# Attention weights times values: a two-part sum against a plain float32 one in two column halves, with dense and grid heads in turn

## The chip, the core and the metric

One core of one Trainium2 chip runs the whole program. The metric is the device time in microseconds (us), from one launch to its end. The core has five engines that run side by side and wait for each other by semaphores: TensorE (PE: matmuls, with PEld for its weight loads), VectorE (DVE), ScalarE (ACT), GpSimd (POOL) and SyncE (SP, which here only starts DMA transfers).

## The reference

The kernel computes a two-layer encoder over 1024 positions of width 1024. In each layer a norm and a projection give queries, keys and values for 16 heads of three kinds; each kind's output is normed, projected and added to x; then comes an MLP.

```python
def reference(x, g_mix, w_in, q_norm, w_uq, kv_norm, w_ukv, rpb, ...):
    for l in range(DEPTH):                                   # DEPTH = 2
        h = rms_norm(x, g_mix[l])
        proj = h @ w_in[l]
        ...
        o_a = dense_attention(qa, ka, kva[..., QK_NOPE:])    # 6 heads, 1024 x 1024, latent keys
        o_b = dilated_sliding_attention(...)                 # 6 heads, three windows with one softmax
        o_c = neighbourhood_attention(..., rpb[l])           # 4 heads on a 16 x 64 grid, bias rpb
        mixed = jnp.concatenate([rms_norm(o_a), rms_norm(o_b), rms_norm(o_c)], axis=-1)
        x = x + mixed @ w_out[l]
        h2 = rms_norm(x, g_mlp[l])
        x = x + jnp.square(jax.nn.relu(h2 @ w_mlp_in[l])) @ w_mlp_out[l]
    return rms_norm(x, g_final)

def dense_attention(q, k, v):
    ...
    sc = jnp.einsum('bqhd,bkhd->bhqk', q_blk, k) * scale
    p = jax.nn.softmax(sc, axis=-1)
    return jnp.einsum('bhqk,bkhd->bqhd', p, v)               # the weighted sum
```

All of it is float32, and each head is 64 wide.

## The kernel before

**Split numbers.** Most matmuls are of type float32r. So that nothing is lost, an operand is kept as two float32r parts: `hi`, which ACT rounds from the float32 value by a copy, and `lo`, which DVE makes as value minus `hi` (helper `rest`, L824). The transposes of probabilities (L1264) and the `merge` (L1304) are plain float32 matmuls.

**Stages of a layer.** Projections (L1174; three passes over hi and lo), then attention, then the norm of its output, the output projection, a second norm and the MLP. The layer loop is a hardware loop (`Fori`) on every engine, so that a wait's target is a register's value worked out with `l`.

**Attention** is a list of 128 items per layer: a head and a block of 128 queries. `HEADS` sets their order: 6 heads of kind A (dense), 6 of kind B (dilated, computed densely with a table of biases), 4 of kind C (grid). A and B items (96 per layer, "dense" below) have 1024 keys, C items (32 per layer) 384. PE's order is written out in the loop of L1308 to L1316. In step i it does:

- `scores(i)` (L1247 for dense, L1238 for grid) into one of two pairs of PSUM banks
- `turns(i - 2)` (L1264): the probabilities of item i-2, turned in blocks of 128x128, 8 for a dense item (two groups of four), 3 for a grid item (one group)
- in every fourth step, `merge` of a block of four items that is done
- `weigh(b, part)`, the weighted sum: a block b of four items is done in four parts, one per step, so that step i holds a quarter of the block of items 4 to 8 places back

In between, DVE takes the row maximum (A: L974) or adds the bias and takes the minimum (B, C: L986), ACT takes the exponential (L716), for C items DVE divides by the sum (L992, L994), and after the turn ACT copies a group to `pT` hi (L706) and DVE writes `pT` lo (L824).

**The weighted sum.** Values lie in DRAM as 128 columns per head, 64 hi and 64 lo, and the stationary operand of a matmul is a tile of 128 keys by these 128 columns. For each tile of keys two matmuls follow, one for each part of `pT`. Rows 0 to 63 of the result hold what the values' hi gives, rows 64 to 127 what lo gives. ACT copies it to `oT` (L734, L742), and `merge` turns it back and adds the two halves, since its moving operand `pair` is two unit matrices of 64 stacked.

**Values on their way to DRAM.** In the projections each of 24 tiles of values per layer is copied to `vst` hi by ACT (L656) and to lo by DVE (L824, L933), and POOL starts the store (L543).

**Grid heads.** SP loads for each C head 6 pieces of features, 16 pieces of values (L420) and two halves of the bias (L381, 768 KB each); a half is loaded when the bias buffer is free. ACT negates the bias, one item's 384 columns at a time (L726), two items ahead.

## Time and profile before

| | us |
|---|---|
| median of 3 runs | 2985.09 |
| lowest and highest run | 2983.09, 2988.78 |
| profiled execution: span, first to last instruction | 2983.4 |
| profiled execution: attention of layer 0, dense items (291.7 to 588) | 296.3 |
| profiled execution: attention of layer 0, grid items (588 to 657) | 69.0 |

Only the span of the profiled execution is recorded, without what lies around it. It is 1.7 us below the median of the runs. The engines' busy shares of the span are PE 96%, DVE 58%, ACT 36%, POOL 1%. A PE that is busy is not always fast: its clock is granted in two levels, shown as a share of full speed, and the mean over the span is 0.983.

How to read the rows further on: a row of instruction groups has line, engine, operation, operands, shape, count, busy time in all, mean duration of one, and the idle time of the engine just before them with what ended it. PE's matmuls overlap each other, so the duration of one is longer than the step from one to the next; a step is read from the starts of two rows of the timeline, divided by the count. A float32 (not float32r) matmul that is no transpose stands in the trace as two records; L1304 is written 256 times and has 512.

### The profile page before, as it was taken

How to read it: one execution, taken by the hardware profiler on the slowest of the kernel's cores; microseconds unless marked ns; L12 is line 12 of the kernel's file. 1: busy time of each engine (PE TensorE's matmuls, PEld its weight loads, DVE VectorE, ACT ScalarE, POOL GpSimd, SP SyncE). 2: the span in 40 equal slices, each digit the busy share in tenths (PEclk: the TensorE clock that was granted, in tenths of full speed). 3: DMA queues.
4: the chain of work that ended last, by engine and by line, in shares of the span. 5: the costliest groups of instructions: out<-in, count | busy, mean ns of one | idle time of the engine just before them, and what ended most of it. 6: DMA issues, size and time to landing. Idle time of an engine off the chain costs nothing.

```text
span 2983.4 us, 43794 instructions
## 1 busy us (share of the span) xinstructions
PE 2876.5 (96%) x14640; PEld 2454.8 (82%) x14640; DVE 1733.5 (58%) x3038; ACT 1081.0 (36%) x2056; POOL 26.5 (1%) x53
## 2 busy tenths in 40 slices
PE   7999999979999999999999999999799999999998
PEld 7998888867888888888799988887688888888886
DVE  5642778865555455455656337788655555455457
ACT  5332768864311111111334236777632111111113
POOL 0000000000000000000000000000000000000000
PEclk9999999989999999999999999999799999999999
DMA  5657534463111111111146573336530111111111
GB/s 192 185 179 181 123 84 94 103 160 120 43 43 56 42 42 56 42 56 49 59 166 200 168 182 88 87 93 142 133 108 29 56 42 56 42 43 55 42 61 69
DMA packets 194043, 281.45 MB, mean 94 GB/s; under 512 B 47184, under 2 KB 153296, under 8 KB 184144
## 3 DMA queue, kind: packets, MB, share of 16 engines
q1 hardware_dynamic: 190032, 262.56, 30.5%
q0 software_dynamic: 3840, 16.78, 1.5%
q8 instruction: 87, 1.43, 0.2%
q14 instruction: 84, 0.69, 0.1%
HBM read 208.50 MB, written 70.78 MB: 94 GB/s over the span
## 4 chain that ended last, share of the span: by engine, by line
PE 83%; DVE 5%; issue 5%; DMA 4%; ACT 2%; DVEq 1%; ACTq 0%; SPq 0%; POOLq 0%
PE ps L1349 23%; PE ps L1174 19%; PE ps L1364 17%; PE ps L1247 7%; PE ps L1264 6%; PE ps L1293 6%; DMA biasC<-in_bias_c 2%; PE ps L1304 2%; PE ps L1211 1%; PE ps L1142 1%; DVE hn L841 1%; DVE x L1095 1%; DMA values<-vst 1%; DVE vbuf L1082 1%; ACT rbuf L774 1%
## 5 line engine op out<-in xcount | busy, mean ns | idle before, releaser
L1364 PE MATMUL ps<-w_dn,hid 128*128 128x512 f32 x3072 | 713.1, 391 | 1.4
L1349 PE MATMUL ps<-hT,w_up 128*128 128x512 f32 x3072 | 702.6, 389 | 3.1 <-DVE hT L824 3.1
L1364 PEld LDWEIGHTS ps<-w_dn,hid 128*128 128x128 f32 x3072 | 573.5, 188 | 132.1 <-DVE x L1095 14.0
L1349 PEld LDWEIGHTS ps<-hT,w_up 128*128 128x128 f32 x3072 | 576.1, 188 | 123.1 <-DVE hT L824 3.6
L1174 PE MATMUL ps<-ws,hT 128*128 128x384 f32 (+3 forms) x3072 | 607.8, 356 | 6.8 <-DVE ws L824 3.5
L1174 PEld LDWEIGHTS ps<-ws,hT 128*128 128x128 f32 x3072 | 535.8, 190 | 53.6 <-issue 6.0
L1095 DVE TENSOR_TENSOR x<-ps,x 128x512 f32<-128x512 f32 x512 | 342.8, 689 | 223.8 <-PE ps L1364 223.4
L1082 DVE TENSOR_TENSOR vbuf<-rbuf 128x512 f32<-128x512 f32 x128 | 88.6, 692 | 367.5 <-ACT rbuf L774 367.5
L824 DVE TENSOR_TENSOR pT<-ps,pT 128x512 fp32r<-128x512 f32 (+1 forms) x448 | 281.6, 664 | 33.5 <-ACT pT L706 33.4
L706 ACT ACTIVATE pT<-ps 128x512 fp32r<-128x512 f32 (+1 forms) x448 | 240.2, 581 | 152.1 <-PE ps L1264 148.0
L774 ACT ACTIVATE rbuf<-ps 128x512 f32<-128x512 f32 x128 | 76.6, 598 | 550.6 <-PE ps L1349 550.6
L760 ACT ACTIVATE w_dn<-raw 128x2048 fp32r<-128x2048 f32 x32 | 61.3, 1917 | 559.0 <-PE ps L1364 559.0
L716 ACT ACTIVATE prob<-ps,a_nm 128x1024 f32<-128x1024 f32 (+1 forms) x256 | 252.5, 986 | 13.5 <-DVE a_nm L986 8.5
L1264 PE MATMUL ps<-ident,prob 128*128 128x128 f32 x1728 | 239.3, 278 | 10.2 <-DVE prob L994 9.4
L1264 PEld LDWEIGHTS ps<-ident,prob 128*128 128x128 f32 x1728 | 204.1, 143 | 51.2 <-issue 20.0
L1247 PE MATMUL ps<-head 128*128 128x512 f32 x768 | 225.7, 395 | 8.6 <-DVEq L935 6.1
L1293 PE MATMUL ps<-pT,head 128*128 128x512 f32 x768 | 224.6, 414 | 0.5 <-DVE pT L824 0.5
L1247 PEld LDWEIGHTS ps<-head 128*128 128x128 f32 x768 | 144.0, 189 | 42.7 <-DVEq L935 6.9
L974 DVE TENSOR_REDUCE a_nm<-ps 128x1 f32<-128x1024 f32 x96 | 117.5, 1224 | 73.3 <-PE ps L1247 72.9
L1293 PEld LDWEIGHTS ps<-pT,head 128*128 128x128 f32 x768 | 130.1, 189 | 17.1 <-issue 0.9
L986 DVE CUSTOM_DVE_ANT_0 ps<-ps,tabB 128x1024 f32<-128x1024 f32 x96 | 118.1, 1230 | 38.5 <-PE ps L1247 36.6
L1142 PE MATMUL ps<-ident,hn 128*128 128x128 f32 x448 | 70.4, 305 | 42.8 <-DVEq L843 22.5
(84 smaller groups left out, 2108.1 us busy)
## 6 DMA issues: line engine op xcount, KB each, us to landing
raw<-in_wstream SPq DMA_DIRECT2D x76, 1024.0 KB, 4.8
head<-feats SPq DMA_DIRECT2D x192, 256.0 KB, 5.8
feats<-tst SPq DMA_DIRECT2D x128, 192.0 KB, 2.6
values<-vst POOLq DMA_DIRECT2D x32, 384.0 KB, 3.1
head<-values SPq DMA_DIRECT2D x24, 512.0 KB, 3.9
biasC<-in_bias_c SPq DMA_DIRECT2D x16, 768.0 KB, 7.3
raw<-in_wstream SPq DMA_DIRECT2D x12, 768.0 KB, 5.7
x_park<-x SPq DMA_DIRECT2D x16, 512.0 KB, 9.1
```

Of the source, the lines that this page charges most:

```text
L706: act.activation(pT[:, b % 2, HI, k0:k0 + nk, (it % 4) * P:(it % 4 + 1) * P], ps[:, 4 + g % 2, 0:nk * P].rearrange("p (k s) -> p k s", s=P ...
L716: act.activation(prob[:, i % 2, 0:wd], s_in, ACT.Exp, bias=a_nm[:, i:i + 1], scale=1.0 if kind == "A" else -1.0, accum_out=a_den[:, i:i + ...
L824: return dve.tensor_tensor(out_lo, full, words(hi), ALU.subtract)
L986: dve.tensor_tensor_reduce(out=s_in, in0=s_in, in1=bias, scale=1.0, scalar=-NEG, op0=ALU.add, op1=ALU.min, accum_out=a_nm[:, i:i + 1])\
L1082: dve.tensor_tensor(vbuf[:, k % 2, :], rbuf[:, k % 2, :], rbuf[:, k % 2, :], ALU.mult)
L1095: dve.tensor_tensor(x[:, s, cols], ps[:, 2 + m % 4, :], x[:, s, cols], ALU.add)\
L1174: last = pe.matmul(out_, a, b, start=(n == 0), stop=(n == len(mms) - 1))
L1247: last = pe.matmul(ps[:, b0 + kh, :], a, b, start=(k == 0), stop=(k == len(mm) - 1))
L1264: last = pe.transpose(ps[:, 4 + g % 2, j * P:(j + 1) * P], prob[:, i % 2, c:c + P], ident[:, :])
L1293: last = pe.matmul(bank, hb[:, 4096 + kt * P:4096 + (kt + 1) * P], pT[:, b % 2, w, kt, :], start=(part == 0 and kt == 0 and w == 0), stop= ...
L1349: last = pe.matmul(ps[:, k % 2, :], w_up[0 if first else 1][:, w1, kt, ft * P:(ft + 1) * P], hT[:, w2, kt, sh * 512:(sh + 1) * 512], start ...
L1364: last = pe.matmul(ps[:, 2 + m % 4, :], hid[slot][:, w1, ft, s * P:(s + 1) * P], w_dn[1 if last_group else 0][:, w2, ft, nh * 512:(nh + 1) ...
```

## The change

Four edits in one.

**1. The weighted sum in plain float32.** Values are stored as 64 float32 columns per head (`vst`, `values`, `v_dense`, `v_grid`), without hi and lo, and `pT` has one float32 part. A matmul of `weigh` has a stationary operand of 64 columns, and its result goes to rows 0 to 63 or to rows 64 to 127 of the bank, in turns: even tiles of keys to the one, odd tiles to the other (grid items: column blocks 0 and 1 to the one, 2 and 3 to the other). In the built program these matmuls carry a tile of the array of 128x64, at column 0 or 64; all others use the whole array. `merge` is as before: it now adds the sum over even tiles to that over odd ones. A group of turned probabilities is copied once, by ACT (`on_act`: first group of a dense item, every group of a grid item) or by DVE (second group of a dense item). The values' tiles on their way to DRAM are copied by ACT alone.

**2. Order of heads.** A0 C0 A1 C1 A2 C2 A3 C3 A4 A5 B0 ... B5.

**3. The bias** is negated by GpSimd, a half of four items (1536 columns) in one instruction.

**4. The layer loop** is a Python loop on all engines, so the program holds both layers one after the other and waits have constants. The loop inside the MLP stays.

```diff
@@ -78,10 +78,15 @@
-HEADS = [("A", h) for h in range(HA)] + [("B", HA + h) for h in range(HB)] + [("C", HA + HB + h) for h in range(HC)]
+HEADS = []
+for h_ in range(HC):
+    HEADS += [("A", h_), ("C", HA + HB + h_)]
+HEADS += [("A", h_) for h_ in range(HC, HA)] + [("B", HA + h_) for h_ in range(HB)]
+GRID_ITEM0 = [8 * n_ for n_, (kind_, _) in enumerate(HEADS) if kind_ == "C"]
+GRID_BEFORE = [sum(kind_ == "C" for kind_, _, _ in ITEMS[:n_]) for n_ in range(NI)]
...
@@ -234,7 +239,7 @@
-    vst = sb("vst", [P, 2, 6, 2 * HD], f32r, "R0", 18 * KB)
+    vst = sb("vst", [P, 2, 6, HD], f32, "R0", 18 * KB)
...
@@ -244,7 +249,9 @@
-    pT = sb("pT", [P, 2, 2, 8, 512], f32r, "H")
+    pT = sb("pT", [P, 2, 8, 512], f32, "H")
+    v_dense = [sb(f"v_dense{k}", [P, 8, HD], f32, "WS", (32 - 32 * k + 16) * KB) for k in range(2)]
+    v_grid = [sb(f"v_grid{k}", [P, 16, HD], f32, "WS", (32 - 32 * k + 16) * KB) for k in range(2)]
...
@@ -404,20 +410,18 @@
-                hb = words(head[k][:, :])
-                    sp.dma_start(hb[:, 4096:5120].rearrange("p (t d) -> p t d", d=P),
-                                 values[:, h * P:(h + 1) * P].rearrange("(t p) d -> p t d", p=P))\
+                    sp.dma_start(v_dense[k][:, :, :],
+                                 values[:, h * HD:(h + 1) * HD].rearrange("(t p) d -> p t d", p=P))\
-                            dst = hb[32 * rr:32 * rr + 32, 3072 + 512 * cb:3072 + 512 * (cb + 1)]
-                            src = grid[rr:rr + 13:4, c_cols(cb):c_cols(cb) + CKC, h * P:(h + 1) * P]
-                            sp.dma_start(dst.rearrange("c (g d) -> c g d", d=P),
+                            src = grid[rr:rr + 13:4, c_cols(cb):c_cols(cb) + CKC, h * HD:(h + 1) * HD]
+                            sp.dma_start(v_grid[k][32 * rr:32 * rr + 32, 4 * cb:4 * cb + 4, :],
...
@@ -447,7 +451,7 @@
-            with sp.Fori(0, DEPTH) as l:
+            for l in range(DEPTH):
...
@@ -501,7 +505,7 @@
-                    if n == 2:
+                    if n == 1:
...
@@ -534,14 +538,19 @@
-            with pool.Fori(0, DEPTH) as l:
+            for l in range(DEPTH):
-                    pool.wait_ge(acc_free_dve, l * DVE_FREE_N + frees_before(ACCS.index(e) + 1, False))
+                    pool.wait_ge(acc_free_act, l * ACT_FREE_N + frees_before(ACCS.index(e) + 1, True))
-                    pool.dma_start(values[e[2] * P:(e[2] + 1) * P, h0 * P:(h0 + nh) * P],
-                                   words(vst[:, k, 0:nh, :].rearrange("p h d -> p (h d)"))).then_inc(vst_out[k], 16)
+                    pool.dma_start(values[e[2] * P:(e[2] + 1) * P, h0 * HD:(h0 + nh) * HD],
+                                   vst[:, k, 0:nh, :].rearrange("p h d -> p (h d)")).then_inc(vst_out[k], 16)
+                for half in range(2 * HC):
+                    pool.wait_ge(biasc_in[half % 2], (l * HC + half // 2 + 1) * 16)
+                    hold(pool)
+                    bias = biasC[half % 2][:, :, :]
+                    pool.tensor_scalar(bias, bias, -1.0, None, ALU.mult).then_inc(biasc_neg, 1)
...
@@ -653,9 +662,9 @@
-                            act.activation(vst[:, vt % 2, 0:nh, 0:HD],
+                            act.activation(vst[:, vt % 2, 0:nh, :],
-                               .then_inc(v_hi, 1)
+                               .then_inc(acc_free_act, 1)
...
@@ -701,11 +710,12 @@
-                            act.wait_ge(t_done, l * NGR + g + 1)
-                            nk, k0 = group_keys(g)
-                            act.activation(pT[:, b % 2, HI, k0:k0 + nk, (it % 4) * P:(it % 4 + 1) * P],
-                                           ps[:, 4 + g % 2, 0:nk * P].rearrange("p (k s) -> p k s", s=P), ACT.Copy)\
-                               .then_inc(t_hi, 1)
+                            if on_act(g):
+                                act.wait_ge(t_done, l * NGR + g + 1)
+                                nk, k0 = group_keys(g)
+                                act.activation(pT[:, b % 2, k0:k0 + nk, (it % 4) * P:(it % 4 + 1) * P],
+                                               ps[:, 4 + g % 2, 0:nk * P].rearrange("p (k s) -> p k s", s=P),
+                                               ACT.Copy).then_inc(pt_act, 1)
...
@@ -718,19 +728,14 @@
-                    n4, part = divmod(i + 2 - 8 * (HA + HB), 4)
-                    if 0 <= n4 < 2 * HC:
-                        if part == 0:
-                            act.wait_ge(biasc_in[n4 % 2], (l * HC + n4 // 2 + 1) * 16)
-                        bias = biasC[n4 % 2][:, part, :]
-                        act.activation(bias, bias, ACT.Copy, scale=-1.0).then_inc(biasc_neg, 1)
-                                act.wait_ge(mg_done, l * NMG + merges_before(b - 1))
+                                after_grid = b % 2 == 0 and ITEMS[4 * b - 4][0] == "C"
+                                act.wait_ge(mg_done, l * NMG + merges_before(b if after_grid else b - 1))
...
@@ -927,13 +932,6 @@
-                        elif e in VSTAGED:
-                            dve.wait_ge(v_hi, l * len(VSTAGED) + vt + 1)
-                            nh = wd // HD
-                            rest(vst[:, vt % 2, 0:nh, HD:2 * HD], bank[:, 0:wd].rearrange("p (h d) -> p h d", d=HD),
-                                 vst[:, vt % 2, 0:nh, 0:HD])
-                            dve.drain().then_inc(acc_free_dve, 1)
-                            vt += 1
...
@@ -978,8 +976,8 @@
-                                n4 = (i - 8 * (HA + HB)) // 4
-                                dve.wait_ge(biasc_neg, l * 8 * HC + i - 8 * (HA + HB) + 1)
+                                n4 = GRID_BEFORE[i] // 4
+                                dve.wait_ge(biasc_neg, l * 2 * HC + n4 + 1)
...
@@ -996,13 +994,15 @@
+                        if it % 4 == 0 and b >= 2:
+                            dve.wait_ge(pv_done, l * NB + b - 1)
-                            dve.wait_ge(t_hi, l * NGR + g + 1)
-                            nk, k0 = group_keys(g)
-                            cols = slice((it % 4) * P, (it % 4 + 1) * P)
-                            rest(pT[:, b % 2, LO, k0:k0 + nk, cols],
-                                 ps[:, 4 + g % 2, 0:nk * P].rearrange("p (k s) -> p k s", s=P),
-                                 pT[:, b % 2, HI, k0:k0 + nk, cols]).then_inc(t_lo, 1)
+                            if not on_act(g):
+                                dve.wait_ge(t_done, l * NGR + g + 1)
+                                nk, k0 = group_keys(g)
+                                dve.tensor_copy(pT[:, b % 2, k0:k0 + nk, (it % 4) * P:(it % 4 + 1) * P],
+                                                ps[:, 4 + g % 2, 0:nk * P].rearrange("p (k s) -> p k s", s=P))\
+                                   .then_inc(pt_dve, 1)
...
@@ -1252,12 +1252,14 @@
-                        pe.wait_ge(pn_ready, l * 8 * HC + i - 8 * (HA + HB) + 1)
+                        pe.wait_ge(pn_ready, l * 8 * HC + GRID_BEFORE[i] + 1)
-                        if g >= 2:
-                            pe.wait_ge(t_lo, l * NGR + g - 1)
+                        if g >= 2 and on_act(g - 2):
+                            pe.wait_ge(pt_act, l * copies(NGR, True) + copies(g - 1, True))
+                        elif g >= 2:
+                            pe.wait_ge(pt_dve, l * copies(NGR, False) + copies(g - 1, False))
...
@@ -1279,20 +1282,20 @@
-                        c, w = part // 2, part % 2
+                        c = part // 2
-                        for n, (g, a, z) in enumerate(((1, 0, 256), (2, 0, 256), (0, 0, 128), (3, 128, 256))):
-                            v = hb[:, 3072 + (4 * cb + g) * P:3072 + (4 * cb + g + 1) * P]
-                            last = pe.matmul(bank[:, c * 256 + a:c * 256 + z], v,
-                                             pT[:, b % 2, w, g, c * 256 + a:c * 256 + z],
-                                             start=(w == 0 and n == 0), stop=(w == 1 and n == 3),
-                                             skip_group_check=True)
+                        for g, a, z in (((1, 0, 256), (2, 0, 256)), ((0, 0, 128), (3, 128, 256)))[part % 2]:
+                            half = 0 if g < 2 else 64
+                            last = pe.matmul(bank[half:half + 64, c * 256 + a:c * 256 + z],
+                                             v_grid[(b // 2) % 2][:, 4 * cb + g, :],
+                                             pT[:, b % 2, g, c * 256 + a:c * 256 + z],
+                                             start=(part % 2 == 0), stop=(part % 2 == 1), skip_group_check=True)
-                            for w in range(2):
-                                last = pe.matmul(bank, hb[:, 4096 + kt * P:4096 + (kt + 1) * P],
-                                                 pT[:, b % 2, w, kt, :], start=(part == 0 and kt == 0 and w == 0),
-                                                 stop=(part == 3 and kt == 7 and w == 1))
+                            half = 64 * (kt % 2)
+                            last = pe.matmul(bank[half:half + 64, :], v_dense[(b // 2) % 2][:, kt, :],
+                                             pT[:, b % 2, kt, :], start=(part == 0), stop=(part == 3),
+                                             skip_group_check=True)
...
@@ -1413,6 +1416,16 @@
+
+
+def on_act(g):
+    it, half = GROUPS[g]
+    return ITEMS[it][0] == "C" or half == 0
+
+
+def copies(n, act):
+
+    return sum(on_act(g) == act for g in range(n))
```

Where instructions stand now is shown at three places. Names: `ps` is PSUM, `ident` the unit matrix, `head` holds queries and keys, `pT` the turned probabilities, `v_dense` and `v_grid` the values, `pair` the moving operand of merge.

PE, in the middle of the A head that comes first, before: one step of the loop, and the start of the next.

```order
L1247 MATMUL ps<-head_83 128x512 x2
L1247 MATMUL ps<-kR,head_83 128x512
L1247 MATMUL ps<-head_83 128x512 x2
L1247 MATMUL ps<-kR,head_83 128x512
L1260 REGISTER_ALU
L1264 MATMUL ps<-ident,prob 128x128 x4
L1260 REGISTER_ALU
L1264 MATMUL ps<-ident,prob 128x128 x4
L1293 MATMUL ps<-pT,head_83 128x512 x4
L1226 REGISTER_ALU
L1247 MATMUL ps<-head_84 128x512 x2
```

The same place in the changed program (here x2 counts matmuls as they are written, each of which is two records when it runs):

```order
L1247 MATMUL ps<-head_83 128x512 x2
L1247 MATMUL ps<-kR,head_83 128x512
L1247 MATMUL ps<-head_83 128x512 x2
L1247 MATMUL ps<-kR,head_83 128x512
L1266 MATMUL ps<-ident,prob 128x128 x8
L1296 MATMUL ps<-pT,v_dense_92 64x512 x2
L1247 MATMUL ps<-head_83 128x512 x2
```

Four matmuls on the whole array between the transposes and the next scores have become two on half of its columns each, and the register instructions are gone.

PE, where the scores of the last block of dense items end and those of grid items begin; before this is behind the last B head:

```order
L1238 MATMUL ps<-head_83 128x384 x2
L1260 REGISTER_ALU
L1264 MATMUL ps<-ident,prob 128x128 x4
L1260 REGISTER_ALU
L1264 MATMUL ps<-ident,prob 128x128 x4
L1293 MATMUL ps<-pT,head_84 128x512 x4
L1226 REGISTER_ALU
L1238 MATMUL ps<-head_83 128x384 x2
```

In the changed program it is behind each of the first four A heads (shown behind the first):

```order
L1266 MATMUL ps<-ident,prob 128x128 x8
L1296 MATMUL ps<-pT,v_dense_92 64x512 x2
L1238 MATMUL ps<-head_84 128x384 x2
L1266 MATMUL ps<-ident,prob 128x128 x8
L1296 MATMUL ps<-pT,v_dense_92 64x512 x2
L1238 MATMUL ps<-head_84 128x384 x2
L1266 MATMUL ps<-ident,prob 128x128 x8
L1296 MATMUL ps<-pT,v_dense_92 64x512 x2
L1238 MATMUL ps<-head_84 128x384 x2
L1266 MATMUL ps<-ident,prob 128x128 x3
L1296 MATMUL ps<-pT,v_dense_92 64x512 x2
```

Between grid items' scores stand the dense head's parts of the weighted sum for six steps; likewise grid parts stand between a dense head's scores afterwards.

ACT, between two grid items, before:

```order
L726 ACTIVATE biasC_88<-biasC_88 128x384
L704 REGISTER_ALU
L706 ACTIVATE pT<-ps 128x3x128
L712 REGISTER_ALU
L716 ACTIVATE prob,a_den<-ps,a_nm 128x384
L726 ACTIVATE biasC_88<-biasC_88 128x384
```

POOL, in the changed program, behind the stores of values of layer 0:

```order
L547 DMA values<-vst 128x384 x16
L547 DMA values<-vst 128x256 x8
L553 ISA
L553 TENSOR_SCALAR biasC_88<-biasC_88 128x1536
L553 TENSOR_SCALAR biasC_89<-biasC_89 128x1536
```

The four negations of 384 columns that ACT did for half a head have become one of 1536 columns on POOL.

## Rows read from the trace of the kernel before

**Rows 1.** the page: busy times, PE's clock in 40 slices, last chain

```profile
PE 2876.5 (96%) x14640; PEld 2454.8 (82%) x14640; DVE 1733.5 (58%) x3038; ACT 1081.0 (36%) x2056; POOL 26.5 (1%) x53
...
PEclk9999999989999999999999999999799999999999
...
PE 83%; DVE 5%; issue 5%; DMA 4%; ACT 2%; DVEq 1%; ACTq 0%; SPq 0%; POOLq 0%
```

**Rows 2.** by stretch: length, PE, PEld, DVE, ACT, POOL, clock, DMA share, GB/s

```profile
291.70:588.00 296.30, 295.34 (x1771) 254.50 (x1770) 239.24 (x376) 222.16 (x406) 0.00 (x0) 1.00 0.42 101
588.00:657.00 69.00, 56.09 (x339) 46.56 (x338) 50.10 (x165) 50.15 (x140) 0.00 (x0) 0.90 0.87 200
2062.00:2133.40 71.40, 57.15 (x338) 47.51 (x337) 50.10 (x164) 50.18 (x139) 0.00 (x0) 0.88 0.85 193
```

**Rows 3.** timeline of PE, dense items: start, length, line, operands, count

```profile
326.80 1.04 PE L1264 MATMUL ps<-ident,prob 128*128 128x128 f32 x8
327.60 1.17 PE L1293 MATMUL ps<-pT,head 128*128 128x512 f32 x4
328.61 0.62 PE L1247 MATMUL ps<-head 128*128 128x512 f32 x2
...
333.15 1.04 PE L1264 MATMUL ps<-ident,prob 128*128 128x128 f32 x8
334.02 1.00 PE L1304 MATMUL ps<-pair,oT 128*128 128x64 f32 x8
334.84 1.17 PE L1293 MATMUL ps<-pT,head 128*128 128x512 f32 x4
```

**Rows 4.** PE's groups by shape: count, busy time, mean ns of one, idle before

```profile
L1264 PE MATMUL ps<-ident,prob 128*128 128x128 f32 x1728 | 239.3, 278 | 10.2 <-DVE prob L994 9.4 <-DVE pT L824 0.6
L1247 PE MATMUL ps<-head 128*128 128x512 f32 x768 | 225.7, 395 | 8.6 <-DVEq L935 6.1 <-ACT prob L716 1.9 <-DMA head<-feats 0.6
...
L1247 PEld LDWEIGHTS ps<-head 128*128 128x128 f32 x768 | 144.0, 189 | 42.7 <-DVEq L935 6.9 <-ACT prob L716 2.8 <-issue 0.8
...
L1174 PE MATMUL ps<-ws,hT 128*128 128x256 f32 x384 | 47.0, 284 | 0.0
```

**Rows 5.** timeline of PE, float32r matmuls of 256 columns in the projections

```profile
261.68 5.99 PE L1174 MATMUL ps<-ws,hT 128*128 128x256 f32 x48
267.51 0.60 PE L1211 MATMUL ps<-ident,stage 128*128 128x128 f32 x4
```

**Rows 6.** timeline of PE, one grid item and the start of the next

```profile
648.58 0.58 PE L1238 MATMUL ps<-head 128*128 128x384 f32 x2
648.99 0.52 PE L1264 MATMUL ps<-ident,prob 128*128 128x128 f32 x3
649.26 0.66 PE L1286 MATMUL ps<-pT,head 128*128 128x256 f32 x4
649.81 0.45 PE L1238 MATMUL ps<-head 128*128 128x384 f32 x1
```

**Rows 7.** waits, grid items of layer 0: total, times, longest

```profile
ACT biasC L726 <- DMA biasC<-in_bias_c: 15.1, 6, 3.9
...
PE ps L1238 <- ACT prob L716: 6.9, 3, 2.5
```

**Rows 8.** ACT's and DVE's groups by shape in the whole run

```profile
L824 DVE TENSOR_TENSOR pT<-ps,pT 128x512 fp32r<-128x512 f32 x384 | 246.1, 682 | 0.8 <-ACT pT L706 0.8
...
L716 ACT ACTIVATE prob<-ps,a_nm 128x1024 f32<-128x1024 f32 x192 | 215.4, 1122 | 10.3 <-DVE a_nm L986 5.6 <-DVE a_nm L974 4.7
...
L726 ACT ACTIVATE biasC<-biasC 128x384 f32<-128x384 f32 x64 | 33.5, 523 | 32.0 <-DMA biasC<-in_bias_c 32.0
```

**Rows 9.** DMA issues by line: count, KB each, us to landing

```profile
head<-feats SPq DMA_DIRECT2D x192, 256.0 KB, 5.8
...
biasC<-in_bias_c SPq DMA_DIRECT2D x16, 768.0 KB, 7.3
```

**Rows 10.** timeline of SP's DMA issues, pieces of values of a grid head

```profile
638.94 5.67 SPq L420 DMA_DIRECT2D head<-values  x12
```

24 lines of the change are left out of this document (12 added, 12 removed).

## The prediction, made before the run

> **What bounds the kernel now.** I read the page first [rows 1]: PE is busy 96% of the span and is 83% of the chain that ended last, while DVE and ACT stand at 58% and 36%. So a term counts by what it does to PE, unless PE waits at that place. Then the stretches of attention [rows 2]. Among the dense items of layer 0 PE is busy for all but 1 of 296.3 us, at full clock: 96 items, 3.09 us each, PE-bound. Among grid items PE is busy 56 of 69 us at a mean clock of 0.90, and the DMA engines are busy 87% at 200 GB/s. The waits say what PE lacks [rows 7]: ACT stood 15.1 us for the bias to land, in six waits, and PE in turn for ACT's exponentials. DVE's and ACT's own work, about 50 us each, would fit in less. The stretch holds 31 starts of grid items: 69.0 / 31 = 2.23 us per item, and 71.4 / 31 = 2.30 in layer 1.
>
> **Durations.** Step of a plain float32 record: 8 transposes of 128 columns from 333.15 to 334.02 [rows 3], 0.109 us each. A float32r matmul of 256 columns has a step of 5.83 / 48 = 0.121 [rows 5]; their mean durations, 278 and 284 ns, are alike as well [rows 4]. So a plain float32 record takes about twice as long per column as float32r, and a matmul that is no transpose has two records. A record of 512 columns then takes 4 x 0.109 = 0.44 us, and a matmul two of these.
>
> A dense part now: from 326.80 to 328.61 stand 8 transposes and the 4 matmuls of `weigh` [rows 3]; 1.81 less 0.87 is 0.94 us. A grid item without merge takes 649.81 - 648.58 = 1.23 us of PE: scores 0.41, transposes 0.33, so its part 0.49 [rows 6]. Merges add 16 records per 8 items at 0.82 / 8 each [rows 3], 0.21 per item. In all 1.44 at full clock, of the 2.23 to 2.30 that the item takes.
>
> **Edit 1, the weighted sum.** A dense part becomes two matmuls, an even tile of keys on the left half of the array and an odd one on the right, each with a hi and a lo record of its stationary operand: in the queue L, L, R, R. What the trace doesn't show is whether the halves run side by side, and what it costs to go from the whole array to a half and back. In every row that I read PE starts matmuls in the program's order, and two records on one half can't share it. Then only the middle two (second L, first R) can overlap: three steps, 3 x 0.44 = 1.32. The bounds are two steps, 0.88 (side by side all along), and four, 1.76 (one after the other). I take three, from the order in the queue.
>
> The Trainium skill, "TensorE: Matmul & The Clock Gate", section "The mechanism", says that matmuls on different tiles of the array start some 4 ns apart, but strictly first in, first out. By that rule it is three steps; no row here shows it.
>
> Price of a switch between whole array and half: at least 0, which is what going from transposes to `weigh` costs now. At most what stands when the array has to run empty and the next weights load only then: a matmul of 512 columns takes 0.395 [rows 4] at a step of 0.94 / 4, so 0.16 from step to end, and a weight load takes 0.189 [rows 4]: 0.35 us. I take 0.16, the first of these two, since weights are loaded beside the matmuls now (PEld is busy 82% beside PE's 96% [rows 1]). Two switches per part: 0.32.
>
> The Trainium skill, "TensorEngine Tiling (Array Packing)", section "Key Properties", says that changing the tiling mode drains TensorE. By it the price is above nothing, without it nothing; the trace of before has no such change.
>
> Dense part: 1.32 + 0.32 = 1.64 us, 0.70 more. Over 192 dense items in two layers: **+134 us**. Nothing hides it, since PE is the bound there.
>
> Grid part: by turns two matmuls of 256 columns (three steps of 0.22) or of 128 (three of 0.11), mean 0.50, with two switches 0.82. A grid item's PE time is 1.44 - 0.49 + 0.82 = 1.77.
>
> The copies: of a dense item's two subtractions of 0.68 us DVE keeps one instruction as a copy, which I price by the same row, and ACT loses one of its two copies. Worth nothing: PE takes 3.09 + 0.70 = 3.8 us per dense item, while ACT, with 1.12 for the exponential and a copy, and DVE stay near 2 [rows 8]. The subtractions of `vst` that go lie under PE's projections, at nothing too.
>
> **Edits 2 and 3, order and bias.** What a C head loads (six pieces of 256 KB and two of 768 KB [rows 9], 16 pieces of values of 32 KB) now has an A head of 8 x 3.8 = 30 us in front. An A head's 2.3 MB (six pieces of 256 KB, four of 128, values of 256) need 12 us at 200 GB/s and have about 19: six of a C head's eight steps hold a dense part (the second pair of order listings), 2.6 us each. So the waits for DMA go, and what is late next is PE; ACT even loses 0.52 per item with the negation [rows 8]. A grid item then costs PE's 1.77: (2.23 - 1.77) x 32 + (2.30 - 1.77) x 32 = **-32 us**. The clock's share is in it, since 1.44 is at full clock.
>
> POOL's negation of 1536 columns has no row. Four of ACT's take 4 x 0.52 = 2.1 us [rows 8], the nearest; I take 3, with ends 1.5 and 10. The bias's second half is issued behind 16 pieces of values, which wait until about the sixth item of the A head. From there to the fifth grid item there are about 3 x 3.8 + 4 x 2.6 = 22 us, less 16 x 0.47 = 8 for issuing [rows 10] and 7 for landing [rows 9]: 7 left. At 3 us the negation is hidden; at 10 it costs 3 us or more per C head, and with late features I put the end at 5, for 8 heads 40 us.
>
> **Edit 4.** The register instructions run ahead of the waits on PE; a few lie in chains (norms, grid items). I take -3 us, from 0 to -10; fetching a longer program may cost as much.
>
> **Sum.** 134 - 32 - 3 = +99. On the profiled span of 2983.4 that is 3082; the median of the runs is 1.7 above that span, so 3084.
>
> **Rivals.**
> - *Full pairing.* The halves run side by side all along. For it: they have their own columns and result rows, and the two matmuls don't depend on each other. Against it: L, L, R, R in a queue that keeps its order. With switches of 0.08 a dense part is 0.88 + 0.16 = 1.04, +19; a grid part 0.33, the item 1.28, -63; with -3 the time is 2985 - 47 = **2938**, faster. Its ends are 2897 (free switches) and 2979 (0.16 each). It decides the sign when a dense part is below about 1.2: there the grid heads' gain outweighs it.
> - *No overlap.* Four steps: dense part 2.08, +219; grid part 0.98, item 1.93, -21; **3180**.
> - *Dear switches.* Three steps and 0.35 per switch: dense part 2.02, +207; grid item 2.15, -8; **3181**. Against it: weights are loaded ahead now.
> - *The order does not pay.* Grid items still wait, for the bias from POOL or for features: 40 more, **3124**. Against it: the slack above.
>
> **How the numbers follow.** Forecast 0.50; its own range goes by the switch from 0 (dense part 1.32, +73; grid item 1.45, -52: 3003) to 0.3 (3155). Full pairing 0.22, no overlap 0.13, dear switches 0.10, the order 0.05. A measurement of this kernel can't tell less than 0.2% (6 us) from no change. Faster: full pairing but for its dear end, and a little of what lies below the forecast, 0.23. Same 0.03. Slower 0.74. The range leaves out the cheapest end of full pairing and the top of the two dear cases: 2935 to 3190.
>
> **What the profile would show.** From the first record of a dense part to the start of the next scores: 1.5 to 1.8 us if I am right, near 1.0 for full pairing, about 2 for the dear cases. Second L and first R with starts a few ns apart for three steps, 0.44 apart for four. An extra gap behind the last transpose and behind the last R is the switch. Grid items with no wait for the bias, and PE at full clock from the first score to the last merge. POOL's negation from 1.5 to 5 us. Dense stretches without idle PE. I am wrong if a dense part costs under 1.2 us, or if DVE or ACT keep PE waiting there.

## The result, and the profile after

The changed kernel takes 3006.3 us (median of four runs, 3001.2 to 3008.4) against 2986.9 for the kernel before beside it: a ratio of 1.0061, interval 1.0047 to 1.0076. It is slower, the way that was forecast, but by 19 us and not by 99. The profiled span is 3003.8, 20.4 more than before.

The page of the changed kernel: busy times, PE's clock, the chain that ended last, and one DMA row [rows 1, 9].

```profile
PE 2918.6 (97%) x14640; PEld 2328.1 (78%) x14640; DVE 1589.7 (53%) x2734; ACT 979.2 (33%) x1800; POOL 91.8 (3%) x69
...
PEclk9999999999999999999999999999999999999999
...
PE 86%; DVE 5%; issue 3%; DMA 2%; ACT 2%; DVEq 1%; SPq 0%; POOL 0%; ACTq 0%; POOLq 0%
...
biasC<-in_bias_c SPq DMA_DIRECT2D x16, 768.0 KB, 6.7
```

DVE and ACT lose 144 and 102 us of work, yet their shares of the chain stay at 5% and 2%; DMA's went from 4% to 2%. Most waits of grid heads for DMA are gone. What is left is at the first grid head of each layer: there DVE waits 6.4 and 5.8 us for the negated bias, whose load was issued at 293.4 us and ready for POOL only at 306.9. POOL's work has risen from 26.5 to 91.8 us.

The time went into attention. From the first score to the start of the last merge matmul, layer 0 takes 403.6 us where it took 382.3, and layer 1 397.8 where it took 389.8. The projections of layer 1 are 4.1 shorter and the start of layer 1 is 3.4 shorter; the rest is within 1.5.

The same view as [rows 2], of two stretches: A and C heads by turns, then dense heads alone (length, PE, PEld, DVE, ACT, POOL, clock, DMA share, GB/s).

```profile
300.00:480.00 180.00, 168.33 (x931) 108.21 (x930) 105.17 (x207) 96.03 (x207) 32.69 (x8) 0.95 0.58 139
480.00:588.00 108.00, 108.00 (x609) 70.38 (x607) 62.53 (x98) 62.57 (x107) 0.00 (x0) 1.00 0.31 69
```

Dense heads alone keep PE busy to the last at full clock. In the mixed heads PE idles for 12 of 180 us, and its clock has a mean of 0.95 (0.90 among the grid items before): something new holds it there, though DVE, ACT and the DMA engines have room.

The dense item in PE's timeline, answering [rows 3].

```profile
577.07 1.08 PE L1296 MATMUL ps<-pT,v_dense 128*64 128x512 f32 x4
578.08 1.19 PE L1247 MATMUL ps<-head 128*128 128x512 f32 x4
579.11 1.03 PE L1266 MATMUL ps<-ident,prob 128*128 128x128 f32 x8
580.07 1.08 PE L1296 MATMUL ps<-pT,v_dense 128*64 128x512 f32 x4
```

From the first record of a part to the next scores is 1.01 us; I had forecast 1.64. The same timeline cut to two moments of one part says why:

```profile
570.22 0.65 PE L1296 MATMUL ps<-pT,v_dense 128*64 128x512 f32 x2
...
570.70 0.60 PE L1296 MATMUL ps<-pT,v_dense 128*64 128x512 f32 x2
```

The four records start at 570.224, 570.231, 570.704 and 570.711: two pairs 7 ns apart, and the next score at 571.233. When all four go to one half they follow each other at 0.43 us or more ("One half per part" below), so each pair is one of L and one of R. The halves run side by side from start to end, in two steps.

What is new between A and C heads shows in the groups by shape [rows 4, 8], mean ns behind the busy time:

```profile
L1003 DVE COPY pT<-ps 128x512 f32<-128x512 f32 x192 | 131.3, 684 | 5.4 <-PE ps L1266 5.0
L553 POOL TENSOR_SCALAR biasC<-biasC 128x1536 f32<-128x1536 f32 x16 | 65.4, 4086 | 268.5 <-DMA biasC<-in_bias_c 268.5
L992 DVE TENSOR_SCALAR prob<-prob,a_rd 128x384 f32<-128x384 f32 x64 | 47.1, 735 | 5.9 <-issue 0.6
L984 DVE CUSTOM_DVE_ANT_0 ps<-ps,biasC 128x384 f32<-128x384 f32 x64 | 36.1, 564 | 70.8 <-PE ps L1238 58.6 <-POOL biasC L553 12.2
```

The negation takes 4.09 us. DVE's scaling of a C item's probabilities (L992), 0.42 us each in the kernel before, has a mean of 0.735. The timeline of all engines around one negation shows where that comes from:

```profile
406.42 0.42 DVE L992 TENSOR_SCALAR prob<-prob,a_rd 128x384 f32<-128x384 f32 x1
...
406.73 4.09 POOL L553 TENSOR_SCALAR biasC<-biasC 128x1536 f32<-128x1536 f32 x1 [14.76 <-DMA biasC<-in_bias_c]
406.76 0.68 DVE L1003 COPY pT<-ps 128x512 f32<-128x512 f32 x1
...
408.13 0.57 DVE L984 CUSTOM_DVE_ANT_0 ps<-ps,biasC 128x384 f32<-128x384 f32 x1 [0.69 <-PE ps L1238]
...
408.86 2.17 DVE L992 TENSOR_SCALAR prob<-prob,a_rd 128x384 f32<-128x384 f32 x1
...
410.95 0.55 DVE L984 CUSTOM_DVE_ANT_0 ps<-ps,biasC 128x384 f32<-128x384 f32 x1
...
411.08 0.55 PE L1266 MATMUL ps<-ident,prob 128*128 128x128 f32 x3 [1.28 <-DVE prob L992]
...
411.65 0.42 DVE L992 TENSOR_SCALAR prob<-prob,a_rd 128x384 f32<-128x384 f32 x1
```

The scaling that starts during POOL's instruction lasts until 411.03, 0.21 us after POOL's end at 410.82; PE waits for it. The copy and the bias addition, which also start during it but read PSUM, keep their lengths. Eight scalings in the run are held so, up to 3.9 us, 20.2 us in all. Nothing in the program connects the two instructions: the one works on the bias, the other on probabilities.

The waits in 300 to 480, where [rows 7] had ACT 15.1 us behind the bias (engine, line, what for: total, times, longest):

```profile
POOL biasC L553 <- DMA biasC<-in_bias_c: 135.3, 8, 23.7
...
PEld ps L1266 <- DVE prob L992: 10.0, 8, 3.3
```

POOL waits for the bias instead of ACT, which costs nothing by itself behind the first grid head, and PE waits for the scaling.

### The profile page after: what moved, and what is told of

Same layout as the page of the kernel before. It is cut to its first block, busy times and chain, and to the rows that moved or that the text cites. A ratio compares the mean times of both kernels' runs of the same rounds, so it can differ in the third digit from the quotient of the medians.

```text
span 3003.8 us, 39412 instructions
## 1 busy us (share of the span) xinstructions
PE 2918.6 (97%) x14640; PEld 2328.1 (78%) x14640; DVE 1589.7 (53%) x2734; ACT 979.2 (33%) x1800; POOL 91.8 (3%) x69
## 4 chain that ended last, share of the span: by engine, by line
PE 86%; DVE 5%; issue 3%; DMA 2%; ACT 2%; DVEq 1%; SPq 0%; POOL 0%; ACTq 0%; POOLq 0%
PE ps L1352 23%; PE ps L1174 20%; PE ps L1367 17%; PE ps L1247 8%; PE ps L1296 6%; PE ps L1266 6%; PE ps L1307 2%; PE ps L1142 1%; PE ps L1211 1%; PE ps L1238 1%; PE ps L1289 1%; DVE x L1095 1%; DMA biasC<-in_bias_c 1%; DMA values<-vst 1%; DVE prob L992 1%
## 5 line engine op out<-in xcount | busy, mean ns | idle before, releaser
L1266 PEld LDWEIGHTS ps<-ident,prob 128*128 128x128 f32 x1728 | 204.4, 141 | 57.3 <-DVE prob L992 18.4
L1247 PE MATMUL ps<-head 128*128 128x512 f32 x768 | 244.4, 419 | 1.8 <-ACT prob L726 1.4
L1247 PEld LDWEIGHTS ps<-head 128*128 128x128 f32 x768 | 129.2, 188 | 134.1 <-issue 112.1
L716 ACT ACTIVATE pT<-ps 128x512 f32<-128x512 f32 (+1 forms) x256 | 146.1, 571 | 249.9 <-PE ps L1266 249.8
L1296 PE MATMUL ps<-pT,v_dense 128*64 128x512 f32 x768 | 211.2, 631 | 0.1
L1003 DVE COPY pT<-ps 128x512 f32<-128x512 f32 x192 | 131.3, 684 | 5.4 <-PE ps L1266 5.0
L1142 PEld LDWEIGHTS ps<-ident,hn 128*128 128x128 f32 x448 | 58.0, 156 | 55.0 <-DVEq L848 36.8
```

Source lines behind the costliest of these rows:

```text
L716: act.activation(pT[:, b % 2, k0:k0 + nk, (it % 4) * P:(it % 4 + 1) * P], ps[:, 4 + g % 2, 0:nk * P].rearrange("p (k s) -> p k s", s=P), A ...
L1003: dve.tensor_copy(pT[:, b % 2, k0:k0 + nk, (it % 4) * P:(it % 4 + 1) * P], ps[:, 4 + g % 2, 0:nk * P].rearrange("p (k s) -> p k s", s=P))\
L1142: last = pe.transpose(ps[:, 6 + hf, k * P:(k + 1) * P], hn[:, t % 2, (4 * hf + k) * P:(4 * hf + k + 1) * P], ident[:, :])
L1247: last = pe.matmul(ps[:, b0 + kh, :], a, b, start=(k == 0), stop=(k == len(mm) - 1))
L1266: last = pe.transpose(ps[:, 4 + g % 2, j * P:(j + 1) * P], prob[:, i % 2, c:c + P], ident[:, :])
L1296: last = pe.matmul(bank[half:half + 64, :], v_dense[(b // 2) % 2][:, kt, :], pT[:, b % 2, kt, :], start=(part == 0), stop=(part == 3), ski ...
```

## The experiments

Theory A after the first look at the two traces: the pairing is full, the new sum costs 0.28 us per dense item, 54 us in all, and the other edits give some 34 back. Its rivals: the sum in halves is free and the new order loses the 19 us (B); or a record of 64 columns is just fast, and the halves never run side by side (C). Theory D, that GpSimd holds VectorE, came only after the first four experiments. Each ratio is against runs of the kernel before on the same chip; three chips served, with medians of that kernel of 2984.0 (e1 to e4, in the order in which they were run), 2985.1 (e5 to e8) and 2982.5 (e9 to e12). The result itself stood beside 2986.9, so differences between experiments of different groups are good to some 4 us.

### Edit 1 undone (e1)

The difference from the changed kernel in outline, not in the code's own lines:

```diff
-    values [SEQ, NH * HD] f32;     pT [P, 2, 8, 512] f32;     two matmuls per part, one per column half
+    values [SEQ, NH * 2 * HD] f32; pT [P, 2, 2, 8, 512] f32r; four matmuls per part, on the whole array
```

> The changed kernel with edit 1 undone: the weighted sum in two float32r parts on the whole array, as before, with the new order of heads, the bias on GpSimd and the layer loop written out. Theory A (new, from the two traces): the plain float32 sum costs PE 0.28 us more per dense item, 54 us in all, and the other edits gave some 34 back. Then this kernel takes 2950 us (2940 to 2962), faster than both. Theory B: the sum in halves is free, and the loss of 19 us comes from the new order (waits for the bias from GpSimd, half-clock stretches): then it stays at 3000 to 3010. My prediction's step (three steps per part) would have it at 2950 as well, but only with a changed kernel at 3084.

2982.65 (ten runs), ratio 0.9995 [0.9986, 1.0005]: no gain that is clear of noise from edits 2 to 4, so 2950 was wrong. The scaling's mean is 735 ns here too, the held time again 20.2 us, and six stretches of half clock (27 us together) lie in attention. PE was busy 164.79 of the 180 us from 300 to 480. The hold is no matter of edit 1.

### The written-out loop alone (e2)

```diff
-            with pe.Fori(0, DEPTH) as l:
+            for l in range(DEPTH):
```

> The kernel before with edit 4 alone. Theory A: the 3.4 us between the last MLP matmul of layer 0 and the first projection of layer 1 go, since the engines no longer start a loop round there, and little else: -4 us (-2 to -6), 2983. Rival: the waits with constants help in every chain of layer 1 as well (the projections of layer 1 got 4.1 us shorter): -8 to -12, 2976. My prediction had -3.

2975.18, ratio 0.9967 [0.9953, 0.9982]: -8.9, at the rival's value. In the profiles (span -4.6, since the profiled execution was the slowest of the five) 3.4 us go between the last MLP matmul of layer 0 and the first projection of layer 1, and 7.4 in the two attentions; the projections give 4.8 back, and what follows attention 1.4. I did not follow these to single instructions, so where the gain of the other executions lies is open.

### The float32 sum alone, in the order of before (e3)

```diff
-                                 for w in range(2):
-                                     last = pe.matmul(bank, hb[:, 4096 + kt * P:4096 + (kt + 1) * P], pT[:, b % 2, w, kt, :], ...)
+                                 half = 64 * (kt % 2)
+                                 last = pe.matmul(bank[half:half + 64, :], v_dense[(b // 2) % 2][:, kt, :], pT[:, b % 2, kt, :], ...)
```

> The kernel before with edit 1 alone: plain float32 weighted sum in column halves, old order of heads, bias negated by ACT, layer loop as before. Theory A: +54 us for 192 dense items at 0.28 each, less some 5 to 15 among the grid items, where values are half the bytes and ACT and DVE have less to do: 3028 (3015 to 3042). Theory B (the sum is free): 2980 to 2987.

3013.78, ratio 1.0099 [1.0082, 1.0115]: +29.7, just below my range. Eight items of an A head (timed here and below from ACT's exponentials) went from 27.2 to 29.5 us and of a B head from 23.5 to 25.7, so 0.28 to 0.29 per item, and the two layers' dense heads take 46 more. Grid heads stay as they were (their wait for DMA is still there). The end of the last block is 2.8 and 4.3 us shorter, and so are the 5.7 and 6.4 us from a layer's first score to its first exponential, by 2.9 and 3.6: 14 us at the two ends of attention that edit 1 gives back.

### One half per part (e4)

The same tiles and records, but both tiles of a part on one half: parts 0 and 2 on the left, parts 1 and 3 on the right. It sums the same products.

```diff
-                            half = 64 * (kt % 2)
+                            half = 64 * (part % 2)
```

(with the sum's start and stop moved to match)

> The changed kernel, with both matmuls of a dense part on the same column half (parts 0 and 2 left, parts 1 and 3 right), same arithmetic and same number of switches. If the halves run side by side now (theory A), this takes it away: a dense part goes from two record steps to four, +0.88 us, times 192: 3175 us. If the halves never ran side by side and a record of 64 columns is just fast (rival C), it stays at 3006.

3141.98 (one run, with a profile). The dense item, PE's timeline:

```profile
578.03 1.03 PE L1266 MATMUL ps<-ident,prob 128*128 128x128 f32 x8
578.99 1.93 PE L1296 MATMUL ps<-pT,v_dense 128*64 128x512 f32 x4
580.86 1.21 PE L1247 MATMUL ps<-head 128*128 128x512 f32 x4
```

The part takes 1.86 us where it took 1.01, its four records 0.48, 0.43 and 0.43 apart. B heads went from 25.7 to 32.7 us, 0.875 per item, which is two record steps. So a record of 512 columns on one half costs 0.43, what I had estimated for the whole array from transposes (4 x 0.109), and the pairing saves two of four. This rules out rival C. The total rose by 136 and not by my 169. In the C heads, which had idle PE time, the price was partly absorbed: eight steps of a C head hold six dense parts, 5.3 us, and their mean rose from 21.4 to 23.9.

### ACT negates again (e5)

```diff
-                    pool.tensor_scalar(bias, bias, -1.0, None, ALU.mult).then_inc(biasc_neg, 1)
+                        bias = biasC[n4 % 2][:, part, :]
+                        act.activation(bias, bias, ACT.Copy, scale=-1.0).then_inc(biasc_neg, 1)
```

> The changed kernel with edit 3 undone: ACT negates the bias again, one item's 384 columns at a time, two items ahead. Theory D (GpSimd blocks VectorE): DVE's scaling of probabilities (TENSOR_SCALAR, 0.42 us) took 2.2 to 3.9 us wherever one of POOL's 4.1 us negations ran, 20.2 us over what it takes alone in the whole run, and PE waited. Then all scalings take 0.42 again and the time falls by 10 to 22 us: 2990 (2984 to 2996). Rival: the wait is hidden behind PE's own work, or ACT's 0.52 per item puts as much back: 3000 to 3010.

2975.46, ratio 0.9968 [0.9957, 0.998], which is 31 us below the changed kernel and below my range. It is also faster than the kernel before. The mixed stretch and the scaling:

```profile
300.00:480.00 180.00, 179.38 (x1048) 118.69 (x1046) 104.48 (x219) 118.83 (x257) 0.00 (x0) 1.00 0.62 147
```

```profile
L993 DVE TENSOR_SCALAR prob<-prob,a_rd 128x384 f32<-128x384 f32 x64 | 26.9, 420 | 5.9 <-issue 0.6
```

Every scaling takes 0.42, PE is busy 179.4 of 180 us at full clock, and an A with a C head takes 42.3 us where the changed kernel takes 44 to 48. In the changed kernel five stretches of half clock (27 us together) lie in attention, here one of 3.4: PE's clock fell where it had waited, and the piece that is left lies where PE still waits. So edit 3 undoes what the order brings. How much of the 31 is the held time of 20.2 and how much the clock that follows it, these runs don't separate; a third share is the first grid heads, where DVE waited 12.2 us for POOL's long negation and waits 6.9 for ACT's short ones.

### POOL negates in four pieces (e6)

The same work on the same engine, with instructions of 384 columns in place of 1536.

```diff
-                    pool.tensor_scalar(bias, bias, -1.0, None, ALU.mult).then_inc(biasc_neg, 1)
+                    for part in range(4):
+                        bias = biasC[half % 2][:, part, :]
+                        pool.tensor_scalar(bias, bias, -1.0, None, ALU.mult).then_inc(biasc_neg, 1)
```

> The changed kernel, with the negation on GpSimd in four instructions of 384 columns instead of one of 1536. Theory D, in the form that a DVE scaling is held until the running POOL instruction ends: a piece takes some 1.1 to 1.3 us, so no scaling takes over 1.7 us, the excess over 0.42 falls from 20 us to 10 or less, and the time to 2996 (2990 to 3002). Rival (the two share a port by turns and POOL's whole work counts): excess and time stay as they are, 3006.

2971.99, ratio 0.9957 [0.9941, 0.9974]. The groups by shape, and one piece with a scaling in the timeline:

```profile
L555 POOL TENSOR_SCALAR biasC<-biasC 128x384 f32<-128x384 f32 x64 | 74.3, 1185 | 233.9 <-DMA biasC<-in_bias_c 233.7
...
L994 DVE TENSOR_SCALAR prob<-prob,a_rd 128x384 f32<-128x384 f32 x64 | 28.2, 440 | 5.9 <-issue 0.6
```

```profile
353.34 3.54 POOL L555 TENSOR_SCALAR biasC<-biasC 128x384 f32<-128x384 f32 x3 [16.08 <-DMA biasC<-in_bias_c]
...
354.17 0.55 DVE L994 TENSOR_SCALAR prob<-prob,a_rd 128x384 f32<-128x384 f32 x1
```

POOL works longer in all (74.3 us against 65.4) and the kernel is 34 us faster than the changed one, where I expected 10. The longest scaling is 0.63 us, the held time 1.3 us of 20.2. It is therefore not POOL's amount of work that slows DVE: the scaling waits for the end of the POOL instruction that is under way (354.51 here, its own end 354.72), and with short ones it soon gets its turn. This settles it against the rival that a rate is shared, which would have left the loss as it was.

### Fewer switches: two parts, four parts in one step (e7, e10, e11)

```diff
-                    if i >= 6 and (i - 6) // 4 < NB:
-                        weigh((i - 6) // 4, (i - 6) % 4)
+                    if i >= 6 and (i - 6) // 4 < NB and (i - 6) % 4 % 2 == 1:
+                        for part_ in range((i - 6) % 4 - 1, (i - 6) % 4 + 1):
+                            weigh((i - 6) // 4, part_)
```

First on the changed kernel:

> The changed kernel, with two parts of the weighted sum in every second step instead of one in each: same matmuls, half as many switches between the whole array and its halves. Theory A with a switch of 0.16 us: a part costs 0.88 for the records and 0.33 for two switches; half of 256 parts lose 0.33, 42 us: 2964 (2958 to 2975 if PE finds no new wait). Rival (the extra 0.3 us belongs to the records, not to the switch): 3006. Rival (longer bursts make ACT and DVE wait, and then PE): over 2990.

3002.91, ratio 1.0058 [1.0041, 1.0075], where I expected 2964. B heads fell as expected, from 25.7 to 24.7 us; the mixed stretch did not:

```profile
300.00:480.00 180.00, 158.84 (x927) 107.75 (x927) 105.46 (x207) 96.84 (x206) 32.68 (x8) 0.95 0.58 137
```

The scalings are held 24.7 us here, and a C head takes 20 to 26.5 us. So it was run again with the POOL pieces, and with the table of the B heads loaded before the ninth head and no longer at the start of attention:

> The changed kernel with the bias in four pieces (run e6, 2972), the table of B heads later, and two parts of the weighted sum per second step. In run e7 a dense item of kind B fell from 3.21 to 3.09 us, but its grid heads got slower under GpSimd's long instructions. Theory: without those the gain of 0.12 per dense item is there in full, 24 us, and the table gives 2 to 5: 2946 (2938 to 2954). Rival: the longer bursts themselves starve ACT and DVE in grid heads: 2960 to 2970.

2963.94, ratio 0.9935 [0.9916, 0.9955]. And with all four parts of a block in every fourth step:

> As e10, with all four parts of a block in one step: a quarter of the switches of the changed kernel. If only switches count, 0.19 per dense item less than with one part per step, 36 us, and with the table 2932 (2925 to 2942), which would beat the split sum. Rival: a burst of 3.6 us on PE is longer than what ACT and DVE have in hand (two score buffers), PE waits behind it, and it is no better than e10: 2945 to 2975.

2948.66, ratio 0.9885 [0.9858, 0.9912]. B heads take 25.7, 24.7 and 24.2 us with four, two and one visits to the halves per block. Four visits fewer in eight items give 1.0 us and two more 0.5: 0.25 us per visit that is saved. Both runs fell short (2946 and 2932 expected) in the C heads, which take 20.0 and 20.5 us where the pieces alone had 18.4; they came out where the rivals had put them. With two parts per step, 300 to 470, PE's waits and the stretch:

```profile
PE ps L1268 <- DVE prob L994: 10.0, 16, 1.1
```

```profile
300.00:470.00 170.00, 159.98 (x979) 111.49 (x978) 97.94 (x211) 102.59 (x217) 36.58 (x32) 1.00 0.61 147
```

Scalings are hardly held there (0.77 us at most, 2.0 us in all in the run); PE reaches the turn of a C item before its probabilities are ready, in the step behind one that has no weighted sum in it. A longer block of PE work saves switches and takes the cover away from the steps between.

What a visit costs shows where a dense step has none. With two parts per step, PE's timeline:

```profile
521.59 1.03 PE L1268 MATMUL ps<-ident,prob 128*128 128x128 f32 x8
522.38 1.17 PE L1249 MATMUL ps<-head 128*128 128x512 f32 x4
523.38 1.13 PE L1268 MATMUL ps<-ident,prob 128*128 128x128 f32 x8
```

From transposes to transposes this step takes 1.80 us. In the changed kernel a step with one part takes 3.00 (577.07 to 580.07 above). The part's two record steps are 0.86 of the 1.21 between them; 0.35 is left for two switches. That a saved visit gives only 0.25 is because the steps that hold parts now lose 0.09 elsewhere: their 8 transposes take 0.97 us to the merge where they took 0.87. I did not follow that.

### Two left, then two right (e12)

The kernel with two parts per step, with the queue L L L L R R R R by records in each part of eight, in place of L L R R L L R R.

```diff
-                        for kt in (2 * part, 2 * part + 1):
+                        for kt in (part // 2 * 4 + part % 2, part // 2 * 4 + part % 2 + 2):
```

(with the sum's start and stop moved to match)

> As e10, but in a step's two parts both matmuls of the left half come first, then both of the right: in the queue eight records L L L L R R R R instead of L L R R L L R R, same arithmetic. Theory A says that a record of one half overtakes waiting records of the other. If it can pass four of them, the time stays at e10's, within 6 us. If it can pass only the one it passes now, halves stand idle: up to 0.88 us more per pair of parts, 96 pairs, 30 to 85 us more than e10. If PE kept strict order, L L R R would never have been free either, and this would be 7 steps of 0.44 against 5 in e10 or more: 80 us and up.

2964.69 (one run), against 2963.94. PE's timeline:

```profile
563.91 1.94 PE L1298 MATMUL ps<-pT,v_dense 128*64 128x512 f32 x8
565.79 1.21 PE L1249 MATMUL ps<-head 128*128 128x512 f32 x4
```

The eight records start at 563.912 and 563.926, 564.392 and 564.406, 564.821 and 564.835, 565.251 and 565.264: four pairs 14 ns apart, 1.87 us to the next scores, as before the swap. In the order L L R R the pairs are 7 ns apart: the first R starts later by about 3.5 ns for each record ahead of it, and not by a step of 0.43 us for each.

### The order with the sum of before: the best version (e8, e9)

Edit 1 undone, ACT negates, and the table of the B heads before the ninth head.

```diff
+                    if n == 2 * HC:
                         sp.dma_start(tabB[:, :], bias_b).then_inc(tab_in, 16)
```

> The kernel of run e1 (weighted sum in two float32r parts, new order, loop written out) with ACT negating the bias, and the table of B heads loaded before head 9 instead of ahead of the first grid head. Theory D: from 2983 the 20 us of held scalings go, and 3 to 8 us of the wait at the first grid head, together -15 to -25: 2962. Rival: ACT and DVE are fuller here (both copies and subtractions of pT), so that ACT's negation costs as much as it frees: 2978 to 2985.

2946.33 (2944.1 to 2946.7), ratio 0.9868 [0.9852, 0.9884]: faster than both kernels, by 39 us than the kernel before, and 16 below my forecast. Its page:

```profile
PE 2857.6 (97%) x14640; PEld 2435.6 (83%) x14640; DVE 1733.1 (59%) x3038; ACT 1083.7 (37%) x2056; POOL 26.3 (1%) x53
...
PE 84%; DVE 6%; issue 3%; ACT 2%; DMA 2%; DVEq 1%; SPq 1%; ACTq 0%; POOLq 0%
```

DVE and ACT have all the work of before [rows 1], and PE's own is 19 us less, with A heads at 23.2 and C heads at 17.0 to 18.8 us: what was won is the waits for DMA, the clock that had fallen with them, and the 9 us of the written-out loop. The same with POOL's pieces in place of ACT:

> The kernel of run e8 (split sum, new order, loop written out, table of B heads later), with the bias negated by GpSimd in four pieces instead of by ACT. From the pair e5 and e6 (2975 against 2972) I expect 2943 (2938 to 2948). Rival: DVE is fuller here with its subtractions, so that pieces of 1.16 us in its way cost more than ACT's negation: 2948 to 2960.

2946.33, ratio 0.9874 [0.9847, 0.99], within noise of the last and of the four-part float32 version (2948.66). Here who negates is of no account once no long POOL instruction is in the way; with the float32 sum the pieces were 3.5 us ahead of ACT (2972.0 against 2975.5).

## Why the prediction was right in sign and wrong in size

| term | predicted | measured | from |
|---|---|---|---|
| edit 1, the sum | +134 | +30 | alone: 3013.8 - 2984.0; in the new order 2975.5 - 2946.3 = +29, the later table in it |
| edit 2, the order | -32, with edit 3 | -29 | 2975.5 - (3013.8 - 8.9) |
| edit 3, POOL negates | 0 | +31 | 3006.3 - 2975.5 |
| edit 4, the loop | -3 | -9 | alone |
| sum | +99 | +22 | the result by itself: +19 |

The terms are differences of medians from different groups of runs. Edit 2's is what the others leave, so the sum must come near the result; a check that is free of this fails by 6 us: by the terms edits 2 to 4 without edit 1 would give -7, and that kernel gave -1.4.

**What was luck.** The sign is luck. Without edit 3's loss the kernel is faster than the one before (2975.5, ratio 0.9968), as full pairing had it; it is slower by a mechanism that the prediction doesn't have. That 3006 lies in the range, near the cheap end of my three steps (3003), is luck for the same reason: 31 us of held VectorE stand where a third record step was meant to.

**The step that failed** is in edit 1: "Then only the middle two (second L, first R) can overlap: three steps, 3 x 0.44 = 1.32", taken "from the order in the queue". The size of a record's step was right (0.43), and the count was wrong: two steps, as in the rival of full pairing. The rows that I rested on showed matmuls of the whole array; they said nothing on halves. What showed it: the pairs 7 ns apart in the changed kernel, the 0.85 us that leaving the pairing costs, and the kernel with four left records ahead of the right ones, which start together all the same. Four records of half the columns in two steps then take 0.86 us; the four float32r matmuls of before took 0.94 by the prediction's own reading. The streaming is no dearer, and what the dense item loses is the switches.

**The switch** was priced at 0.16 and measured at 0.17 to 0.18 (0.35 for two, from the step without a part above). The dense item's steps, from start to start:

| | before | after |
|---|---|---|
| 8 transposes to the part | 0.790 | 0.965 |
| the part to the next scores | 1.008 | 1.009 |
| scores to transposes, A head | 1.380 | 1.495 |

The sum rose by 0.29: 0.35 for two switches, less what the streaming saves. 0.18 of it stands in front of the part and the rest in the first score matmul behind; the part itself is as long as before because its last switch takes what its records save.

The sum of the rival *Full pairing* was wrong on record: its grid part of 0.33 left the two switches out. With 0.08 each it is 0.49, the item 1.44 and the term -53, so that the rival stood at 2948 with ends 2907 and 2989, and not at 2938 with 2897 and 2979. With the measured 0.35 for two, a dense part is 1.21, +52; a grid part 0.68, the item 1.63, -41; with -3 the sum is +8 and the time 2993. The kernel with everything but edit 3 measured 2975.5, 17 less: 6 are edit 4's, and most of the rest is what edit 1 gave back at the two ends of attention (14 us when alone), which I had put at nothing. So the rival that I gave 0.22 was the right mechanism for edit 1, with the dearer end of its switch.

The Trainium skill, "TensorE: Matmul & The Clock Gate", section "The mechanism", has matmuls of different tiles start in strict order, some 4 ns apart. The starts 7 and 14 ns apart agree in kind; the order does not: by that rule the part would take three steps (four left records then four right: seven), and the traces show two and four. The measurement decides. The Trainium skill, "TensorEngine Tiling (Array Packing)", section "Key Properties", says that a change of tiling mode drains the engine; the trace agrees, at 0.35 us for the way there and back.

**Edit 2** was right in mechanism: the waits for DMA went but for the first grid head of each layer, and grid heads are bound by PE (A with C 42.3 us, PE busy 179.4 of 180 us at full clock) as soon as nothing holds DVE. That -32 and -29 agree is in part luck, since -32 was worked out with three steps per grid part; with the steps and switches as measured the same working gives -41, and why the order gave 12 less is open.

**Edit 3** is the second step that failed, and one that no rival named: it was put at 0 and cost 31 us. "At 3 us the negation is hidden" asked only whether POOL would be done in time, and there 4.09 us was nearly good enough: DVE waited for a negation in the first grid head of each layer, 12.2 us in all, and never after. The bias of the first, in layer 0, had landed 13.5 us behind its issue in place of my 7. What I left out is what a POOL instruction does to DVE while it runs. I had even credited ACT's lost 0.52 per item as a help, where ACT had room.

The Trainium skill, "SBUF — State Buffer", section "Who interferes with whom", says that GpSimd and some VectorE instructions (`tensor_scalar` and copies from SBUF to SBUF among them) need one shared pair of ports, held for a whole instruction, and that the later one blocks. The trace agrees: the held scaling ends 0.21 us after POOL's instruction, and copies from PSUM pass. By this rule edit 3 would have been a rival of its own, at 16 negations of 4 us with a scaling every 2.3 us.

**Edit 4** gave three times what I took, inside my bound of -10. **The copies** that went leave DVE 144 us and ACT 102 us less work and bought nothing among the items, as forecast. Whether the 14 us at the ends of attention come from them no run shows.

## What to carry to other kernels

When independent work is put on column halves, count its steps by the halves' own queues and not by the program's order, and then pay for each entry and exit: here two switches per visit, 192 visits of dense parts, are all that a dense item lost. Before moving a small job to an idle GpSimd, look at which VectorE instructions run beside it and how long its longest instruction is; if it must go there, cut it to the length of what it may delay. And where a change has several parts, price the one that looks free by asking what it holds, not only whether it is done in time.

## What the runs showed of the hardware that I had not expected

- A record for one column half starts beside one of the other half that stands four places ahead of it in the queue (14 ns apart; 7 ns for two places). Two records on one half follow at 0.43 us for 512 columns of float32.
- Going from the whole array to column halves and back cost 0.35 us per visit.
- A VectorE `tensor_scalar` of 384 columns that reads and writes SBUF took up to 3.9 us in place of 0.42 when a GpSimd instruction of 4.09 us was under way. It ended 0.21 us behind it. VectorE instructions that read PSUM kept their time, and so did the small reciprocal (128x1, L990, 0.16 us).
- GpSimd took 4.09 us for a `tensor_scalar` of 128x1536 float32 and 1.19 for one of 128x384; ACT took 0.51 for the latter.
